# Row count of the second score matmul, and one gather and turn of the short request's rows for four experts

## The chip, the cores and the metric

The kernel runs on one core of one Trainium2 chip. The metric is the device time of one execution in microseconds (us). Below, TensorE is called PE in the profile (its weight loads PEld), VectorE DVE, ScalarE ACT, GpSimd POOL; SPq is the queue of DMA issues of SyncE.

## The reference

One encoder layer is applied to two requests that share the weights: a prompt of 256 tokens and a sample of 1024 tokens, 1024 features each. All is float32.

```
h = x @ W_in + b_in                       # 8 attention heads of 64, and 8 gMLP groups
attn = softmax over three dilated windows # = one softmax with a bias row per head
gm   = gelu(u) * (W_s LN(gelu(v)) + b)
x1   = LN(alpha * x + concat(attn, gm) @ W_out)
aff  = softmax(x1 @ w_router)             # 16 experts
gates, idx = top_k(aff.T, cap)            # cap = 32 rows (prompt), 128 rows (sample) per expert
ys   = (silu(xs @ wg) * (xs @ wu)) @ wd   # xs = x1[idx], hidden width 2816
out  = LN(alpha * x1 + scatter_add(ys * gates))
```

## The kernel before

The program is written by hand for each engine, in one fixed order, with semaphores between the engines. Its stages follow each other: input product (45 to 349 us), attention (351 to 688 us), output product with the first layer norm and the router (to about 860 us), choice of the rows for each expert (TensorE nearly idle, to 934 us), and then sixteen experts, 130 us each (942 to 3031 us), and a short end.

Float32 accuracy comes from splitting. A value is written as a high part (a rounded type, `F32R`, which TensorE takes in one pass) and a low part (the rest); ACT makes high parts by a copy, DVE low parts by a subtraction (`low`, line 920).

**Attention.** A unit is one head, one request and one tile of 128 queries; there are 80 units, per head 2 of the prompt (256 keys) and 8 of the sample (1024 keys). A head has 64 features, half of the array's 128 rows. For the even heads the high parts of q lie on partitions 0 to 63 of `q_parts` and its low parts on 64 to 127; for the odd heads the other way round. `k_high` holds the high part of k in both halves. So line 475, `q` times `k_high` with 128 rows, adds high times high and low times high in one matmul. Line 476 adds the high part of q times `k_low`, and reads only the 64 rows of one half: `q[base:base + HD]` and `k_low[base:base + HD, ...]`. A sample unit has two blocks of 512 keys, thus four matmuls: 475, 476, 475, 476; a prompt unit has two of 256 keys. In one turn n of its loop TensorE computes the scores of unit n (475, 476), turns the probabilities of unit n-2 (line 484, eight 128x128 transposes for a sample unit, two for a prompt unit) and multiplies those of unit n-3 with v (line 495, sixteen or four instructions). DVE adds the bias and takes the maximum (line 1005), ACT takes the exponential (771) and copies the turned probabilities (765), DVE normalises the output (1014, 1015). In between, ACT and DVE write the parts of q and k for the next head (746 and 920).

**Experts.** Each expert has 66 weight units of 512 KB that SP loads into a ring of 14. ACT and DVE split each into `w_parts`, and TensorE multiplies the sample request's 128 rows with them in three passes (`gate_up`, `down`), and the prompt's 32 rows with the raw float32 unit (`short_gate_up`, `short_down`; tiles of 128 rows and 32 columns). The rows of expert e+1 are turned in unit 55 of expert e: POOL has gathered 128 rows into `xs` and 32 rows into `xs_p` (named xs_prompt in the profile; the other 96 partitions are zero, line 1109), two indirect DMAs for each expert (1250, 1251). `xs_transposes` turns `xs_p` and `xs` block by block, 8 + 8 transposes (574, 575), into three banks given by `xs_banks`; ACT copies them out in six pieces (812, 813), DVE makes three low parts (`xs_low`).

Of the kernel before, what the change touches and what calls it, by code (L numbers as in the profile page):

```python
# [15 lines left out]
P = 128  # L16
# [71 lines left out]
def build(nc, a, outs):  # L88
# [10 lines left out]
    with ExitStack() as ctx:  # L99
# [73 lines left out]
        xs_parts = place("xs_parts", 32768, 2, KT, CAP_S, dt=F32R)  # L173
        xs_short = place("xs_short", 34816, KT, CAP_P)
        h_parts = place("h_parts", 35328, 2, FT, CAP_S, dt=F32R)
# [13 lines left out]
        fin = place("fin", 14336, FIN_RING, D)  # L189
        fin_stats = place("fin_stats", 19840, 2, 6)  # L190
        out_idx = place("out_idx", 20048, 2)[:, :].bitcast(U32)
        nmr = place("minus_mean_rstd", 52832, TILES)
# [47 lines left out]
        s_hT, s_hh, s_hp, s_hid = sem("hT_done"), sem("hT_high"), sem("hT_short"), sem("hT_low")  # L240
        s_gath = sem("gathered")
        s_xsT, s_xsH, s_xsL = sem("xsT_done"), sem("xs_high"), sem("xs_low")
        s_ys, s_scat = sem("ys_ready"), sem("scattered")
# [52 lines left out]
        def xs_banks(e):  # L296

            return *pair(e - 1, NC - 2), short_bank(e - 1, NC - 1)

# [86 lines left out]
        def _(pe):  # L386
# [75 lines left out]
            for n in range(NU + 3):  # L462
                if n < NU:
                    h, g, qt = units[n]
                    if n >= 2:
                        pe.wait_ge(s_scored, n - 1)
                    if qt == 0:
                        pe.wait_ge(s_sl, len(LOW_STEPS) * h + 2 * (g + 1))
                    base, t0 = HD * (h % 2), gtile[g] * P
                    q = q_parts[:, h % 2, t0 + qt * P:t0 + (qt + 1) * P]  # L470
                    for c in range(0, glen[g], 512):
                        cn = min(512, glen[g])
                        out, ks = psum[:, 2 * (n % 2) + c // 512, 0:cn], slice(t0 + c, t0 + c + cn)

                        nc.tensor.matmul(out, q, k_high[:, h % 2, ks], start=True, stop=False)  # L475
                        last = nc.tensor.matmul(out, q[base:base + HD], k_low[base:base + HD, h % 2, ks], start=False, stop=True)  # L476
                    last.then_inc(s_qk, 1)
# [90 lines left out]

            def xs_transposes(e):


                for k in range(KT):
                    bank, o0 = xs_banks(e)[k // 3], k % 3 * SLOTS
                    nc.tensor.transpose(psum[:, bank, o0:o0 + P], xs_p[:, k * P:(k + 1) * P], ident)
                    last = nc.tensor.transpose(psum[:, bank, o0 + CAP_P:o0 + SLOTS], xs[:, k * P:(k + 1) * P], ident)
                last.then_inc(s_xsT, 1)

            pe.wait_ge(s_idx, 1)
            pe.wait_ge(s_gath, 32)
            xs_transposes(0)  # L580
# [18 lines left out]
            def short_gate_up(e, end):  # L599

                first = BATCH_ENDS[BATCH_ENDS.index(end) - 1] + 1 if end > 3 else 0
                for u in range(first, end + 1, 2):
                    c, ks, _ = chunk_of(u)
                    n, slot = CHUNKS[c][1], (e * UNITS + u) % RING
                    if ks[0] == 0 and c == 1 and e:
                        pe.wait_ge(s_ys, e)
                    elif ks[0] == 0 and c != 1 and e * NC + c >= 2:
                        pe.wait_ge(s_mul_p, e * NC + c - 1 if c else e * NC)
                    for i, k in enumerate(ks):
                        for g in range(4):  # L610
                            last = nc.tensor.matmul(psum[32 * g:32 * g + 32, short_bank(e, c), 0:n // 2].rearrange("p (j f) -> p j f", j=2),  # L611
                                                    xs_short[:, k, :],
                                                    raw[:, slot:slot + 2, i * n + g * (n // 4):i * n + (g + 1) * (n // 4)],
                                                    start=k == 0, stop=k == KT - 1)
                last.then_inc(s_raw, 1)
# [37 lines left out]
            for e in range(EXPERTS):  # L653
                pe.wait_ge(s_xsL, e + 1)
                for u in range(UNITS):
                    pe.wait_ge(s_lo, e * UNITS + u + 1)
# [6 lines left out]
                    if u == XS_TURN_AT and e < EXPERTS - 1:  # L663
                        pe.wait_ge(s_hid, e * NC + NC - 1)
                        pe.wait_ge(s_hp, e * NC + NC - 1)
                        pe.wait_ge(s_mul_p, e * NC + NC)
                        pe.wait_ge(s_gath, e * 32 + 64)
                        xs_transposes(e + 1)
# [5 lines left out]
        def _(act):  # L674
# [132 lines left out]
            def xs_copy(e):  # L807
                act.wait_ge(s_xsT, e + 1)
                for b, bank in enumerate(xs_banks(e)):
                    nk = min(3, KT - 3 * b)  # L810
                    turned = psum[:, bank, 0:nk * SLOTS].rearrange("p (k c) -> p k c", k=nk)
                    nc.scalar.copy(xs_short[:, 3 * b:3 * b + nk, :], turned[:, :, 0:CAP_P])
                    last = nc.scalar.copy(xs_parts[:, HI, 3 * b:3 * b + nk, :], turned[:, :, CAP_P:SLOTS])
                last.then_inc(s_xsH, 1)

            def silu(e, c):
# [78 lines left out]
        def _(dve):  # L895
# [77 lines left out]
            def split_low(step):  # L973
# [8 lines left out]
                else:  # L982
                    low(k_low[here, h % 2, cols], kT[here, h // 2, cols], k_high[here, h % 2, cols]).then_inc(s_sl, 1)

            for step in range(len(LOW_STEPS)):
                split_low(step)
# [121 lines left out]
            nc.vector.tensor_scalar(top_idf[0:EXPERTS, :], top_idf[0:EXPERTS, :], float(L_PROMPT), None, ALU.add).then_inc(s_top, 1)  # L1108
            link(nc.vector.memset(xs_p, 0.0))
            dve.wait_ge(s_topT, 1)  # L1110
# [4 lines left out]
            nc.vector.tensor_copy(idx[:, 2, :], psum[:, 2, 32:48])  # L1115

            nc.vector.tensor_scalar(out_idx[:, 0:1], psum[:, 1, EXPERTS - 1:EXPERTS], -float(L_PROMPT), None, ALU.add).then_inc(s_idx, 1)

            def xs_low(e):
                dve.wait_ge(s_xsH, e + 1)  # L1120
                for b, bank in enumerate(xs_banks(e)):
                    nk = min(3, KT - 3 * b)
                    ks = slice(3 * b, 3 * b + nk)
                    turned = psum[:, bank, 0:nk * SLOTS].rearrange("p (k c) -> p k c", k=nk)
                    last = low(xs_parts[:, LO, ks, :], turned[:, :, CAP_P:SLOTS], xs_parts[:, HI, ks, :])
                last.then_inc(s_xsL, 1)
# [92 lines left out]
        def _(pool):  # L1219
# [108 lines left out]
```

## Time and profile before

| | |
|---|---|
| median of 3 runs | 3056.05 us (3044.93 to 3086.59) |
| profiled execution | 3055.43 us, of which span 3053.6 us |
| busy share of the span | PE 95%, PEld 73%, DVE 61%, ACT 52%, POOL 7% |
| mean granted TensorE clock | 0.963 of full speed |

The page of the profile gives busy time per engine, but a matmul's duration there contains its way through the array, and matmuls overlap. So durations of single matmuls are not their price: the price is the distance from one start to the next. The rows below come from the timeline (start, duration, engine, line, operation, output and inputs; in brackets the idle time before it and what ended it), from the table of stretches (windows), and from the groups of instructions. The row count of a matmul's stationary tile stands before the star: 64*128 is 64 rows and 128 columns. The granted clock is 1.00 at 2.4 GHz and 0.50 at 1.2 GHz.

### The profile page before, as it was taken

The page shows a single profiled execution, that of the slowest core. Times are in us where ns is not written, and L with a number is a line of the kernel's source. Part 1 is how long each engine was busy: PE and PEld are TensorE (multiplying, and loading weights), DVE is VectorE, ACT ScalarE, POOL GpSimd, SP SyncE. Part 2 cuts the span into 40 slices and gives each one's busy share as a digit, 9 for nine tenths or more (in the row PEclk, how much of TensorE's full clock was granted, in tenths as well). Part 3 has the DMA queues.
Part 4 walks back from the last instruction along what each step waited for, and adds up shares of the span by engine and source line. Part 5 has one row for each costly group of instructions (what it writes and reads, how often), then busy time and mean ns, then how long its engine had stood idle before and what let it go on. Part 6 is the DMA issues. An engine that isn't in the chain of part 4 may idle for free.

```text
span 3053.6 us, 50934 instructions
## 1 busy us (share of the span) xinstructions
PE 2903.5 (95%) x21389; PEld 2227.6 (73%) x21389; DVE 1857.0 (61%) x2261; ACT 1573.2 (52%) x2054; POOL 202.7 (7%) x167
## 2 busy tenths in 40 slices
PE   6999999998917999999999999999999999999996
PEld 6998777777715777777777777777777777777774
DVE  3531135545476666666766666666666666666688
ACT  2201346652104666665666666566665666656663
POOL 0200000000000000000000000000000000000054
PEclk8999769999958999999999999999999999999998
DMA  4100101012234787887878878788787878878794
GB/s 153 42 29 14 41 15 37 28 70 81 85 138 155 261 294 271 284 280 260 294 265 287 283 265 287 259 295 276 270 289 256 293 269 292 275 259 293 269 348 181
DMA packets 293217, 636.96 MB, mean 209 GB/s; under 512 B 22547, under 2 KB 68499, under 8 KB 292947
## 3 DMA queue, kind: packets, MB, share of 16 engines
q1 hardware_dynamic: 278544, 599.46, 55.6%
q0 software_dynamic: 9216, 26.87, 3.7%
q10 hardware_dynamic: 5228, 7.36, 0.7%
q8 instruction: 169, 2.77, 0.4%
q14 instruction: 60, 0.49, 0.0%
HBM read 607.34 MB, written 26.28 MB: 207 GB/s over the span
## 4 chain that ended last, share of the span: by engine, by line
PE 90%; DVE 6%; issue 1%; DMA 1%; ACT 0%; POOL 0%; ACTq 0%; DVEq 0%; POOLq 0%
PE banks L635 16%; PE banks L594 11%; PE banks L428 11%; PE banks L611 10%; PE banks L595 10%; PE banks L596 10%; PE banks L648 5%; PE banks L495 4%; PE banks L484 3%; PE banks L476 2%; PE banks L475 2%; PE banks L623 1%; DVE w_parts L920 1%; DMA b_s<-in_gmlp_b_s 1%; DVE top L1097 1%
## 5 line engine op out<-in xcount | busy, mean ns | idle before, releaser
L920 DVE TENSOR_TENSOR w_parts<-raw_units,w_parts 128x1024 fp32r<-128x1024 f32 x1056 | 1292.3, 1233 | 640.0 <-ACT w_parts L874 593.1
L874 ACT CAST w_parts<-raw_units 128x1024 fp32r<-128x1024 f32 x1056 | 1104.9, 1052 | 792.3 <-PE banks L596 490.0
L594 PE MATMUL banks<-w_parts,xs_parts 128*128 128x512 f32 (+1 forms) x1536 | 594.8, 387 | 6.0 <-DVE w_parts L920 6.0
L595 PE MATMUL banks<-w_parts,xs_parts 128*128 128x512 f32 (+1 forms) x1536 | 574.9, 374 | 0.0
L596 PE MATMUL banks<-w_parts,xs_parts 128*128 128x512 f32 (+1 forms) x1536 | 572.3, 373 | 0.0
L635 PE MATMUL banks<-w_parts,h_parts 128*128 128x512 f32 x2112 | 510.6, 397 | 4.0 <-DVE h_parts L920 4.0
L635 PEld LDWEIGHTS banks<-w_parts,h_parts 128*128 128x128 f32 x2112 | 390.8, 189 | 119.3 <-issue 39.8
L594 PEld LDWEIGHTS banks<-w_parts,xs_parts 128*128 128x128 f32 x1536 | 289.7, 189 | 129.1 <-issue 72.0
L611 PE MATMUL banks<-raw_units,xs_short 128*32 128x256 f32 (+1 forms) x6144 | 344.1, 364 | 0.0
L596 PEld LDWEIGHTS banks<-w_parts,xs_parts 128*128 128x128 f32 x1536 | 290.2, 189 | 52.4
L595 PEld LDWEIGHTS banks<-w_parts,xs_parts 128*128 128x128 f32 x1536 | 290.3, 189 | 44.6
L611 PEld LDWEIGHTS banks<-raw_units,xs_short 128*32 128x32 f32 x6144 | 176.2, 110 | 131.1 <-issue 44.5
L1005 DVE CUSTOM_DVE_ANT_0 scored<-banks,relT 128x1024 f32<-128x1024 f32 (+1 forms) x80 | 85.1, 1064 | 169.9 <-PE banks L476 169.6
L428 PE MATMUL banks<-win_parts,x_parts 128*128 128x256 f32 x1440 | 175.8, 286 | 4.5 <-issue 4.5
L428 PEld LDWEIGHTS banks<-win_parts,x_parts 128*128 128x128 f32 x1440 | 175.4, 195 | 4.7 <-issue 4.7
L648 PE MATMUL banks<-raw_units,h_short 128*32 128x256 f32 x2816 | 171.9, 382 | 0.0
L1262 POOL DMA_INDIRECT acc_rows<-ys,idx x15 | 31.4, 2092 | 1784.8 <-ACT ys_prompt L855 1784.8
L495 PE MATMUL banks<-v_rows,probsT 128*128 128x64 f32 x1088 | 144.7, 290 | 0.0
L495 PEld LDWEIGHTS banks<-v_rows,probsT 128*128 128x128 f32 x1088 | 142.9, 211 | 0.0
L765 ACT COPY probsT<-banks 128x1024 f32<-128x1024 f32 (+1 forms) x80 | 70.7, 884 | 134.4 <-PE banks L484 134.2
L648 PEld LDWEIGHTS banks<-raw_units,h_short 128*32 128x32 f32 x2816 | 81.8, 110 | 69.5 <-issue 25.7
L428 PE MATMUL banks<-x_parts,win_parts 128*128 128x512 f32 (+1 forms) x576 | 110.4, 354 | 0.0
(167 smaller groups left out, 2302.9 us busy)
## 6 DMA issues: line engine op xcount, KB each, us to landing
raw_units<-in_w_gate SPq DMA_DIRECT2D x352, 512.0 KB, 5.5
raw_units<-in_w_up SPq DMA_DIRECT2D x352, 512.0 KB, 6.4
raw_units<-in_w_down SPq DMA_DIRECT2D x352, 512.0 KB, 5.7
win_raw<-in_w_in SPq DMA_DIRECT2D x10, 1024.0 KB, 5.1
relT<-rel_bias SPq DMA_DIRECT2D x8, 960.0 KB, 4.3
x_rows<-x SPq DMA_DIRECT2D x10, 512.0 KB, 2.6
acc_rows<-ax SPq DMA_DIRECT2D x10, 512.0 KB, 2.6
fin<-acc_rows POOLq DMA_DIRECT2D x10, 512.0 KB, 8.0
```

The costliest lines, as they stand in the source:

```text
L428: last = nc.tensor.matmul(out, w_of(wp), x_of(xp), start=first and n == 0, stop=last_one and n == 2)
L484: last = nc.tensor.transpose(psum[:, 4 + kt // 4, kt % 4 * P:(kt % 4 + 1) * P], probs[:, m % 3, kt * P:(kt + 1) * P], ident)
L495: last = nc.tensor.matmul(psum[:, 6 + m % 2, 0:HD], probsT[:, m % 2, kt, :], v_rows[:, gtile[g] + kt, h * HD:(h + 1) * HD], start=kt == 0, ...
L594: nc.tensor.matmul(out, xs_parts[:, HI, k, :], w_hi, start=k == 0, stop=False)
L595: nc.tensor.matmul(out, xs_parts[:, LO, k, :], w_hi, start=False, stop=False)
L596: last = nc.tensor.matmul(out, xs_parts[:, HI, k, :], w_lo, start=False, stop=k == KT - 1)
L611: last = nc.tensor.matmul(psum[32 * g:32 * g + 32, short_bank(e, c), 0:n // 2].rearrange("p (j f) -> p j f", j=2), xs_short[:, k, :], raw[ ...
L635: last = nc.tensor.matmul(psum[:, pair(e, NC)[half], :], h_parts[:, h_part, f, :], w_parts[:, w_part, slot, half * 512:half * 512 + 512], ...
L648: last = nc.tensor.matmul(psum[32 * g:32 * g + 32, short_bank(e, NC), 0:QUARTER], h_short[:, f, :], raw[:, (e * UNITS + GU_UNITS + f) % RI ...
L874: nc.scalar.copy(w_parts[:, HI, n % SPLIT, :], raw[:, n % RING, :]).then_inc(s_hi, 1)
L920: return nc.vector.tensor_tensor(out, whole, high.bitcast(F32), ALU.subtract)
L1005: link(nc.vector.tensor_tensor_reduce(out=scored[:, n % 2, 0:L], in0=src, in1=bias, scale=1.0, scalar=-3e38, op0=ALU.add, op1=ALU.max, acc ...
```

## The change

In attention, `k_low` is cleared once where no low part of k is ever written (the 64 other partitions of both buffers), and line 476 takes all 128 rows of q and `k_low`. The products with the zeros add nothing.

In the experts, the rows of the short request are gathered for four experts by one indirect DMA, which fills all 128 partitions of `xs_p`; the row numbers come from a new tile `idx_four`. It is turned only ahead of experts 0, 4, 8 and 12, into two further banks, and copied whole to a larger `xs_short` of 128 columns per block, of which expert e reads the columns of its quarter. The rows of the sample are turned in blocks of four to a bank, so that ACT and DVE have two pieces where they had three. The clearing of `xs_p` goes.

```diff
         def xs_banks(e):
-            return *pair(e - 1, NC - 2), short_bank(e - 1, NC - 1)
+            return *pair(e - 1, NC - 2), pair(e - 1, NC - 1)[1], short_bank(e - 1, NC - 1)
...
                         nc.tensor.matmul(out, q, k_high[:, h % 2, ks], start=True, stop=False)
-                        last = nc.tensor.matmul(out, q[base:base + HD], k_low[base:base + HD, h % 2, ks], start=False, stop=True)
+                        last = nc.tensor.matmul(out, q, k_low[:, h % 2, ks], start=False, stop=True)
...
             def xs_transposes(e):
+                banks = xs_banks(e)
+                pe.wait_ge(s_gath, 16 * (e + 1))
                 for k in range(KT):
-                    bank, o0 = xs_banks(e)[k // 3], k % 3 * SLOTS
-                    nc.tensor.transpose(psum[:, bank, o0:o0 + P], xs_p[:, k * P:(k + 1) * P], ident)
-                    last = nc.tensor.transpose(psum[:, bank, o0 + CAP_P:o0 + SLOTS], xs[:, k * P:(k + 1) * P], ident)
+                    last = nc.tensor.transpose(psum[:, banks[k // 4], k % 4 * P:(k % 4 + 1) * P], xs[:, k * P:(k + 1) * P], ident)
+                if e % 4 == 0:
+                    pe.wait_ge(s_gath_p, 16 * (e // 4 + 1))
+                    for k in range(KT):
+                        last = nc.tensor.transpose(psum[:, banks[2 + k // 4], k % 4 * P:(k % 4 + 1) * P], xs_p[:, k * P:(k + 1) * P], ident)
                 last.then_inc(s_xsT, 1)
...
-                                                    xs_short[:, k, :],
+                                                    xs_short[:, k, e % 4 * CAP_P:(e % 4 + 1) * CAP_P],
...
                     if u == XS_TURN_AT and e < EXPERTS - 1:
                         pe.wait_ge(s_hid, e * NC + NC - 1)
-                        pe.wait_ge(s_hp, e * NC + NC - 1)
+                        pe.wait_ge(s_hp, e * NC + (NC if (e + 1) % 4 == 0 else NC - 1))
                         pe.wait_ge(s_mul_p, e * NC + NC)
-                        pe.wait_ge(s_gath, e * 32 + 64)
                         xs_transposes(e + 1)
...
             def xs_copy(e):
                 act.wait_ge(s_xsT, e + 1)
...
+                for b in range(2):
+                    last = nc.scalar.copy(xs_parts[:, HI, 4 * b:4 * b + 4, :], psum[:, banks[b], :].rearrange("p (k c) -> p k c", k=4))
                 last.then_inc(s_xsH, 1)
+                if e % 4 == 0:
+                    for b in range(2):
+                        last = nc.scalar.copy(xs_short[:, 4 * b:4 * b + 4, :], psum[:, banks[2 + b], :].rearrange("p (k c) -> p k c", k=4))
+                    last.then_inc(s_xsP, 1)
...
+            dve.wait_ge(s_job, len(jobs))
+            nc.vector.memset(k_low[HD:P, 0, :].bitcast(F32), 0.0)
+            link(nc.vector.memset(k_low[0:HD, 1, :].bitcast(F32), 0.0))
             for step in range(len(LOW_STEPS)):
                 split_low(step)
...
-            link(nc.vector.memset(xs_p, 0.0))
...
+            for g in range(4):
+                nc.vector.tensor_scalar(idx_four[32 * g:32 * g + 32, :], psum[32 * g:32 * g + 32, 2, 32 + g:48:4], -float(g), 0.25,
+                                        ALU.add, ALU.mult)
...
             def gather(e):
                 pool.indirect_dma_start(xs, None, x1_d, rows_at(0, e, P)).then_inc(s_gath, 16)
-                pool.indirect_dma_start(xs_p[0:CAP_P, :], None, x1_d, rows_at(1, e, CAP_P)).then_inc(s_gath, 16)
+                if e % 4 == 0:
+                    pool.indirect_dma_start(xs_p, None, x1_d,
+                                            bass.IndirectOffsetOnAxis(ap=idx_four[:, e // 4:e // 4 + 1], axis=0)).then_inc(s_gath_p, 16)
```

Where the order of instructions changes, it stands so. On TensorE, in unit 55 of expert 0 (between the two products of `down` and the short request's), before the change:

```order
L635 MATMUL banks<-w_parts,h_parts 128x512 x24
L574 MATMUL banks<-ident,xs_prompt 128x128
L575 MATMUL banks<-ident,xs 128x128
L574 MATMUL banks<-ident,xs_prompt 128x128
L575 MATMUL banks<-ident,xs 128x128
```

and so on to sixteen transposes. After the change, ahead of expert 1 (and of every expert that is no multiple of four):

```order
L627 MATMUL banks<-ident,hidden 128x128 x2
L628 MATMUL banks<-ident,hidden_short 64x128
L652 MATMUL banks<-raw_units,h_short 32x256 x16
L639 MATMUL banks<-w_parts,h_parts 128x512 x24
L575 MATMUL banks<-ident,xs 128x128 x8
L652 MATMUL banks<-raw_units,h_short 32x256 x16
```

The eight transposes of the short request are gone there; ahead of experts 4, 8 and 12 they stand behind the eight of the sample.

On DVE, where the input product ends and attention starts, after the change (before it, the two rows with MEMSET are not there, and the others follow in the same order):

```order
L926 TENSOR_TENSOR win_parts<-win_raw,win_parts 128x2048 x3
L993 MEMSET k_low 64x1280
L994 MEMSET k_low 64x1280
L926 TENSOR_TENSOR q_parts<-qT_first,q_parts 64x256
L926 TENSOR_TENSOR k_low<-kT,k_high 64x256
```

Two clearings of 1280 columns come ahead of the first low parts.

On POOL's queue, at the start of the experts, after the change:

```order
L1261 DMA xs<-x_rows,idx 128x1024
L1263 DMA xs_prompt<-x_rows,idx_four 128x1024
L1261 DMA xs<-x_rows,idx 128x1024
L1275 DMA acc_rows<-ys,idx 1280x1024
L1276 DMA acc_rows<-ys_prompt,idx 5120x256
L1261 DMA xs<-x_rows,idx 128x1024
```

Before it, every gather of `xs` was followed by one of 32 rows into `xs_p`; now one of 128 rows follows each fourth.

## Rows read from the trace of the kernel before

**Rows 1.** The page: the chain that ended last, shares by engine.
```profile
PE 90%; DVE 6%; issue 1%; DMA 1%; ACT 0%; POOL 0%; ACTq 0%; DVEq 0%; POOLq 0%
```

**Rows 2.** Windows: length; busy PE, PEld, DVE, ACT, POOL; clock; DMA share; GB/s.
```profile
351.10:436.50 85.40, 82.97 (x277) 61.51 (x277) 27.95 (x75) 34.95 (x56) 0.00 (x0) 0.50 0.12 42
436.50:684.00 247.50, 247.50 (x1614) 193.10 (x1614) 124.00 (x351) 151.22 (x230) 0.00 (x0) 1.00 0.11 42
934.40:937.80 3.40, 3.40 (x16) 3.21 (x16) 0.00 (x0) 0.00 (x0) 0.00 (x0) 0.50 0.00 0
937.80:942.30 4.50, 0.20 (x1) 0.03 (x1) 2.63 (x5) 4.20 (x9) 1.81 (x2) 0.88 0.46 143
942.30:948.30 6.00, 6.00 (x14) 4.74 (x15) 6.00 (x6) 4.49 (x6) 0.00 (x0) 0.50 0.01 2
950.00:2980.00 2030.00, 2028.29 (x15976) 1492.68 (x15975) 1389.74 (x1376) 1240.97 (x1558) 142.13 (x91) 1.00 0.81 279
```

**Rows 3.** Timeline, PE: one sample unit at full clock, and the next one's start.
```profile
481.91 0.48 PE L475 MATMUL banks<-k_high,q_parts 128*128 128x512 f32 x1
482.32 0.49 PE L476 MATMUL banks<-k_low,q_parts 64*128 64x512 f32 x1
...
483.61 1.09 PE L484 MATMUL banks<-ident,probs 128*128 128x128 f32 x8
...
486.24 0.48 PE L475 MATMUL banks<-k_high,q_parts 128*128 128x512 f32 x1
```

**Rows 4.** Timeline, PE: one sample unit at the low clock, and the next one's start.
```profile
376.13 0.77 PE L475 MATMUL banks<-k_high,q_parts 128*128 128x512 f32 x1
376.84 0.79 PE L476 MATMUL banks<-k_low,q_parts 64*128 64x512 f32 x1
...
384.04 0.78 PE L475 MATMUL banks<-k_high,q_parts 128*128 128x512 f32 x1
```

**Rows 5.** Timeline, PE: matmuls with 128 rows only, first expert, at either clock.
```profile
943.29 0.63 PE L596 MATMUL banks<-w_parts,xs_parts 128*128 128x512 f32 x1
943.72 0.63 PE L594 MATMUL banks<-w_parts,xs_parts 128*128 128x512 f32 x1
...
949.14 0.39 PE L596 MATMUL banks<-w_parts,xs_parts 128*128 128x512 f32 x1
949.37 0.39 PE L594 MATMUL banks<-w_parts,xs_parts 128*128 128x512 f32 x1
```

**Rows 6.** Timeline, ACT and DVE: one attention unit at full clock, with parts written.
```profile
479.06 1.05 ACT L746 CAST k_high<-kT 64x1024 fp32r<-64x1024 f32 x1
480.40 1.01 ACT L765 COPY probsT<-banks 128x1024 f32<-128x1024 f32 x1 [0.30 <-PE banks L484]
481.44 1.15 ACT L771 ACTIVATE probs<-scored,nmx 128x1024 f32<-128x1024 f32 x1
482.50 0.19 ACT L771 ACTIVATION_READ_ACCUMULATOR probs<-scored,nmx 128x1 f32 x1
483.71 1.23 DVE L1005 CUSTOM_DVE_ANT_0 scored<-banks,relT 128x1024 f32<-128x1024 f32 x1 [1.24 <-PE banks L476]
```

**Rows 7.** Timeline, PE: starts of two units, the first with four products by v.
```profile
470.25 0.48 PE L475 MATMUL banks<-k_high,q_parts 128*128 128x512 f32 x1
473.24 0.48 PE L475 MATMUL banks<-k_high,q_parts 128*128 128x512 f32 x1
```

**Rows 8.** Timeline, PE: the first matmul of attention.
```profile
351.10 0.52 PE L475 MATMUL banks<-k_high,q_parts 128*128 128x256 f32 x1 [2.42 <-DVE k_low L920]
```

**Rows 9.** Groups by form, DVE: the clearing of the short request's tile.
```profile
L1109 DVE MEMSET xs_prompt<- 128x1024 f32 x1 | 0.9, 912 | 0.2 <-issue 0.2
```

**Rows 10.** Timeline, PE: the first of sixteen transposes, and what follows them.
```profile
1052.44 0.27 PE L574 MATMUL banks<-ident,xs_prompt 128*128 128x128 f32 x1
...
1054.28 1.93 PE L648 MATMUL banks<-raw_units,h_short 128*32 128x256 f32 x32
```

**Rows 11.** Timeline, PE: the first turn of all, and the first expert's first matmul.
```profile
934.36 0.45 PE L574 MATMUL banks<-ident,xs_prompt 128*128 128x128 f32 x1 [7.52 <-DMA xs_prompt<-x_rows,idx]
...
942.30 0.77 PE L594 MATMUL banks<-w_parts,xs_parts 128*128 128x512 f32 x1 [4.30 <-DVE w_parts L920]
```

More of the change, by code:

```diff
@@ L173, in build @@
         xs_parts = place("xs_parts", 32768, 2, KT, CAP_S, dt=F32R)
-        xs_short = place("xs_short", 34816, KT, CAP_P)
+        xs_short = place("xs_short", 50368, KT, P)
         h_parts = place("h_parts", 35328, 2, FT, CAP_S, dt=F32R)
@@ L190, in build @@
         fin_stats = place("fin_stats", 19840, 2, 6)
+        idx_four = place("idx_four", 20064, 4)[:, :].bitcast(U32)
         out_idx = place("out_idx", 20048, 2)[:, :].bitcast(U32)
@@ L240, in build @@
         s_hT, s_hh, s_hp, s_hid = sem("hT_done"), sem("hT_high"), sem("hT_short"), sem("hT_low")
-        s_gath = sem("gathered")
-        s_xsT, s_xsH, s_xsL = sem("xsT_done"), sem("xs_high"), sem("xs_low")
+        s_gath, s_gath_p = sem("gathered"), sem("gathered_short")
+        s_xsT, s_xsH, s_xsL, s_xsP = sem("xsT_done"), sem("xs_high"), sem("xs_low"), sem("xs_short")
         s_ys, s_scat = sem("ys_ready"), sem("scattered")
@@ L468, in _ @@
                         pe.wait_ge(s_sl, len(LOW_STEPS) * h + 2 * (g + 1))
-                    base, t0 = HD * (h % 2), gtile[g] * P
+                    t0 = gtile[g] * P
                     q = q_parts[:, h % 2, t0 + qt * P:t0 + (qt + 1) * P]
@@ L569, in xs_transposes @@
             def xs_transposes(e):
+                banks = xs_banks(e)
+                pe.wait_ge(s_gath, 16 * (e + 1))
                 for k in range(KT):
-                    bank, o0 = xs_banks(e)[k // 3], k % 3 * SLOTS
-                    nc.tensor.transpose(psum[:, bank, o0:o0 + P], xs_p[:, k * P:(k + 1) * P], ident)
-                    last = nc.tensor.transpose(psum[:, bank, o0 + CAP_P:o0 + SLOTS], xs[:, k * P:(k + 1) * P], ident)
+                    last = nc.tensor.transpose(psum[:, banks[k // 4], k % 4 * P:(k % 4 + 1) * P], xs[:, k * P:(k + 1) * P], ident)
[3 more added lines that the diff above has]
+                        last = nc.tensor.transpose(psum[:, banks[2 + k // 4], k % 4 * P:(k % 4 + 1) * P], xs_p[:, k * P:(k + 1) * P], ident)
                 last.then_inc(s_xsT, 1)
             pe.wait_ge(s_idx, 1)
-            pe.wait_ge(s_gath, 32)
             xs_transposes(0)
@@ L654, in _ @@
                 pe.wait_ge(s_xsL, e + 1)
+                pe.wait_ge(s_xsP, e // 4 + 1)
                 for u in range(UNITS):
@@ L808, in xs_copy @@
                 act.wait_ge(s_xsT, e + 1)
[L809 to L813, printed above, removed]
+                banks = xs_banks(e)
+                for b in range(2):
+                    last = nc.scalar.copy(xs_parts[:, HI, 4 * b:4 * b + 4, :], psum[:, banks[b], :].rearrange("p (k c) -> p k c", k=4))
                 last.then_inc(s_xsH, 1)
+                if e % 4 == 0:
+                    for b in range(2):
+                        last = nc.scalar.copy(xs_short[:, 4 * b:4 * b + 4, :], psum[:, banks[2 + b], :].rearrange("p (k c) -> p k c", k=4))
+                    last.then_inc(s_xsP, 1)
             def silu(e, c):
@@ L1120, in xs_low @@
                 dve.wait_ge(s_xsH, e + 1)
[L1121 to L1125, printed above, removed]
+                for b in range(2):
+                    ks = slice(4 * b, 4 * b + 4)
+                    last = low(xs_parts[:, LO, ks, :], psum[:, xs_banks(e)[b], :].rearrange("p (k c) -> p k c", k=4), xs_parts[:, HI, ks, :])
                 last.then_inc(s_xsL, 1)
```

## The prediction, made before the changed kernel ran

> **What bounds the kernel now.** I read the chain that ended last first: 90% of it is TensorE [rows 1], so work taken from TensorE shortens the end, wherever TensorE does not wait. Then the windows: from 436.5 to 684 us, most of attention, TensorE is busy for every microsecond at clock 1.00, and from 950 to 2980 us, the experts, for 2028 of 2030 us [rows 2]. DVE and ACT are busy for 50 and 61% in the first stretch, for 68 and 61% in the second. One thing stands out: from 351.1 to 436.5 us the clock is 0.50, though TensorE counts as busy for 83 of the 85.4 us [rows 2]. Last the timeline, since busy time hides what matters here.
>
> A sample unit at full clock takes 486.24 - 481.91 = 4.33 us. Its four score matmuls take 483.61 - 481.91 = 1.70 us, 0.425 us from start to start [rows 3]. Matmuls of the same width and type that all have 128 rows start every 0.23 us (949.14, 949.37) [rows 5]; I take 0.227, the mean over a run of them. So each of the four loses 0.2 us. At the low clock a unit takes 384.04 - 376.13 = 7.91 us with scores at 0.71 to 0.72 [rows 4], where the all-128-row stream has 0.43 [rows 5]: 0.29 us lost each. What differs is that 128 rows and 64 rows alternate. The Trainium skill (TensorEngine Tiling (Array Packing), Key Properties) says that a change of the tiling mode drains TensorE; the trace agrees, with 0.2 us at each change.
>
> **Part 1: scores with 128 rows.** Four matmuls at 0.227 instead of 0.425 save 0.79 us per sample unit, and two save 0.40 us per prompt unit. A head has 8 and 2 of them: 7.1 us; eight heads 57 us. The fourth change of mode, to the transposes behind the scores, is in it, because the 1.70 us ends at the first transpose. The added 64 rows cost nothing by themselves: the distance goes by columns, and the 128-row matmul of line 475 is as long as the 64-row one of line 476 (0.48 and 0.49) [rows 3].
>
> Not all of the 57 us need arrive, for the new unit takes 4.33 - 0.79 = 3.54 us, and ACT in a unit with a 1024-wide part needs 1.05 + 1.01 + 1.15 + 0.19 = 3.40 us [rows 6]. It just fits; DVE had 1.24 us idle in its unit [rows 6] and loses 0.79 of them. But in each head two units have only four products by v instead of sixteen; one lasts 473.24 - 470.25 = 2.99 us [rows 7] and becomes 2.2 us, below ACT's 3.40. The other is shorter still, but ACT has less to do in it. TensorE then waits, by ACT's lag less what its lead gives back. Bounds per head: 0 us (ACT works off its lag in the units without parts, where it needs 2.35 us) and 3 us (both short units last as long as ACT's, and DVE's order adds some). I take 1 us, since an exponential is needed only two units later: 8 us over eight heads.
>
> **Part 2: the low clock at the start of attention.** It costs now 85.4 x (1 - 4.33/7.91) = 38.7 us. What did TensorE do before the clock rose elsewhere? From 934.4 to 937.8 us it ran 16 transposes back to back at 0.50, and then stood at 0.88 on average over the next stretch; from 942.3 to 948.3 it ran dense 128-row matmuls at 0.50, and was at 1.00 after [rows 2]. In attention at the low clock the scores of a unit are not dense: 0.43 us of streaming in 0.72 [rows 4, 5]. With the change a low-clock unit has 4 x 0.43 = 1.7 us of dense scores, then about as long of transposes without a change of mode between them: as much dense work in a row as preceded the rise after 934.4. So I expect the clock to come up in the first few sample units. As an estimate I take 20 us of low clock from the first matmul. A low-clock unit is then 7.91 - 4 x 0.29 = 6.75 us, so the stretch costs 20 x (1 - 3.54/6.75) = 9.5 us. Gain: 29 us. Bounds: the low clock is gone within 5 us (gain 36), or lasts as long as now (cost 85.4 x 0.476 = 40.6, a loss of 2).
>
> **Part 3: the clearing of k_low.** Two MEMSETs of 1280 columns; one of 1024 takes 0.91 us [rows 9], so 2.3 us on DVE ahead of the first low parts, and DVE can only start when the input product ends. TensorE's first matmul waits for k_low [rows 8] and moves by about 1.2 us, because DVE had waited for ACT's high parts anyway. But then TensorE waits for the first maximum, which comes behind the sample's low parts, and these wait for ACT's copies (to about 352.5 us), which are not moved. I take 0; if the cover fails it is 2.3 us.
>
> **Part 4: the turns of the short request.** Sixteen transposes take 1054.28 - 1052.44 = 1.84 us [rows 10], so eight about 0.87 us. They go ahead of 12 of the 16 experts (not 0, 4, 8, 12): 10.4 us. TensorE is the bound there [rows 2], so it all counts. ACT has one block of six copies fewer in those, DVE two subtractions for three; both have room and are taken at nothing. The new wait for `s_hp` ahead of experts 4, 8 and 12 asks for the last hidden copy of ACT, which ACT does behind the split of unit 57, free to run when TensorE has done unit 51; between that and unit 55 lie four `down` units of 1.4 us and one short product, so it is long done. If not, it would be below 2 us three times. Behind it on TensorE stands everything, so it would count in full. Gathering 128 rows in one DMA instead of 32 four times moves the same bytes, issued an expert ahead: nothing.
>
> At the first turn the gather is on the path: TensorE waits 7.52 us for the `xs_p` rows, and starts the experts at 942.30, held by DVE's low part [rows 11]. Now `xs` can be turned while `xs_p` is under way, the clearing (0.91 us [rows 9]) goes, four tiny index operations come, `xs_p` has four times the rows, and ACT copies `xs_short` in two blocks of 512 behind what DVE needs. Bounds: 1.5 us gained, 2 us lost. I take 0.
>
> **The sum.** The profiled execution took 3055.4 us (span 3053.6), 0.6 below the median of the three runs. 3055.4 - 57 + 8 - 29 - 10.4 = 2967 us. The spread of the three runs, 3045 to 3087 us, is of the size of the low stretch's cost, so I think its length varies from run to run; that is not shown by this trace.
>
> **The rivals.**
> - *The low clock stays as long.* For it: TensorE counted as busy in it too, and the products by v (line 495) are unchanged. Against: the rise after transposes alone. Then 3055.4 - 57 + 8 + 2 - 10.4 = 2998 us. The Trainium skill (TensorE: Matmul & The Clock Gate, Part 4) says that transposes don't count as busy for the clock; by that rule this rival would be likely. This trace does not agree: 16 transposes alone, 934.4 to 937.8 us, were followed by a rise [rows 2].
> - *ACT and DVE become the bound in attention.* At 3 us lost per head, 16 more than in my sum: 2983 us. For it: 3.40 against 3.54 us; against: most units have no 1024-wide part.
> - *The change does not do what it says:* the pause belongs to something else that the scores do, such as sharing q as the stationary tile or the switch of banks. Against: the experts' three passes share tiles as well and have no pause [rows 5]. Then only part 4 is left: 3045 us.
> - *Slower:* tighter scores let TensorE wait for ACT in small pieces, and the clock stays at 0.50 for all of attention. Each of the 64 sample units is then 6.75 instead of 3.54 us: 205 us more than at full clock, 196 more than in my sum, 3163 us. It turns from gain to loss when the low stretch costs more than 38.7 + 59 = 98 us, that is after 98/0.476 = 206 us of low clock. Against: from 436.5 us on the clock held at 1.00 with the pauses of today [rows 2], and the new units are denser.
>
> **How the numbers follow.** My forecast 0.58, the low clock as long 0.20, ACT and DVE 0.12, no effect on the scores 0.05, slower 0.05. The predicted time is 2967 us. The low end is the forecast without any wait for ACT (8 us), with the low clock gone in 5 us (7) and the first turn's gain: 2950, and some for the spread of runs, 2945. The high end takes in the rival with the long low clock, 2998, and a few us of unknown costs: 3003. About 2% is what a measurement of this kernel can tell from no change: 2995 us is that line. Faster by over 2%: 0.58 + 0.12 and 0.08 of the 0.20 that lies at the line, 0.78. Within 2%: 0.12 + 0.05 = 0.17. Slower: 0.05.
>
> **What would show it.** The score matmuls start every 0.23 us at full clock and the first transpose follows at the same pace; if they stay at 0.43, part 1 is wrong. A full unit takes 3.5 to 3.6 us. In the windows, the clock reaches 1.00 before 375 us; if it is still 0.50 at 420, part 2 is wrong. TensorE's idle time ahead of lines 475 and 484, put down to ACT's exponential or copy, shows the wait: 8 us in all, not 24. An expert that is no fourth takes 0.87 us less than 130.1 us, and no idle time stands ahead of the turns at unit 55. The prediction fails if the clock behaves otherwise than after the two rises in [rows 2], in either direction.

## The result, and the profile after

The changed kernel takes 2967.1 us (median of 4 runs, 2966.6 to 2967.9); the kernel before took 3050.5 us in the runs beside it (3041 to 3087). The ratio is 0.975, 95% interval 0.971 to 0.979: 2.5% faster. (The two medians alone give 0.973; the ratio is taken over the fast runs.) One thing shows before any trace is opened: the runs of the kernel before spread over tens of us, those of the changed one over 1.2 us.

The page of the changed kernel, its first line, then the lines of the clock and of the chain, which answers to [rows 1]:

```profile
span 2964.8 us, 50663 instructions
...
PEclk9999999999769999999999999999999999999998
...
PE 88%; DVE 7%; DMA 1%; issue 1%; ACT 1%; POOL 0%; ACTq 0%; SPq 0%; DVEq 0%; POOLq 0%
```

TensorE is the bound as before. Where the time went is read from the table of stretches. The stretches run from the first score matmul to the first transpose of the concatenated rows (attention), from there to the first matmul of the experts, through the experts to DVE's last sums (`ys`), and to the end. The columns are start and end, length, busy time and count on PE, PEld, DVE, ACT and POOL, granted clock, DMA share and GB/s. Before:

```profile
351.10:688.12 337.02, 334.02 (x1920) 258.02 (x1920) 152.84 (x430) 187.18 (x286) 0.00 (x0) 0.87 0.11 41
688.12:942.30 254.18, 159.81 (x829) 132.05 (x830) 148.81 (x231) 44.47 (x67) 11.77 (x24) 0.82 0.26 97
942.30:3032.20 2089.90, 2084.14 (x16356) 1534.30 (x16360) 1445.65 (x1428) 1276.21 (x1600) 169.76 (x110) 1.00 0.81 277
3032.20:3053.60 21.40, 0.91 (x16) 0.26 (x8) 11.31 (x16) 0.00 (x0) 4.57 (x6) 0.62 0.09 31
```

After:

```profile
352.00:610.27 258.27, 248.19 (x1921) 230.68 (x1921) 152.43 (x430) 185.26 (x284) 0.00 (x0) 0.99 0.15 52
610.27:864.38 254.11, 160.02 (x830) 131.80 (x830) 148.58 (x233) 44.71 (x65) 10.99 (x23) 0.81 0.27 98
864.38:2944.40 2080.02, 2073.63 (x16260) 1522.34 (x16264) 1444.45 (x1413) 1276.76 (x1546) 157.22 (x99) 1.00 0.81 278
2944.40:2964.80 20.40, 0.93 (x16) 0.27 (x10) 11.31 (x16) 0.00 (x0) 4.56 (x6) 0.64 0.09 32
```

Attention is 78.8 us shorter, the experts 9.9 us, the end 1.0 us; the middle is the same to 0.1 us. As the first score matmul comes 0.9 us later, that is 88.8 us of span. In attention the mean clock went from 0.87 to 0.99. The low stretch of [rows 2], 85 us long before, is at most 7.5 us long now (the first four matmuls, to 352.5 us, still had the clock at 1.00, hence the mean of 0.54):

```profile
352.00:359.50 7.50, 5.30 (x18) 4.05 (x19) 5.01 (x12) 5.46 (x10) 0.00 (x0) 0.54 0.86 280
359.50:607.00 247.50, 240.19 (x1883) 224.07 (x1881) 146.52 (x415) 179.58 (x275) 0.00 (x0) 1.00 0.13 46
```

And the timeline of TensorE at full clock, to be held against [rows 3] (a sample unit and the next one's start; lines 477 and 478 are the old 475 and 476):

```profile
450.39 0.48 PE L477 MATMUL banks<-k_high,q_parts 128*128 128x512 f32 x1
450.71 0.39 PE L478 MATMUL banks<-k_low,q_parts 128*128 128x512 f32 x1
450.94 0.40 PE L477 MATMUL banks<-k_high,q_parts 128*128 128x512 f32 x1
451.17 0.39 PE L478 MATMUL banks<-k_low,q_parts 128*128 128x512 f32 x1
451.40 0.38 PE L486 MATMUL banks<-ident,probs 128*128 128x128 f32 x2
```

The four score matmuls take 1.01 us where they took 1.70. They start 0.23 us apart, but the first takes 0.32 us, behind the products by v. A full sample unit, from 366.65 to 370.25 us, takes 3.60 us instead of 4.33.

### The profile page after: what moved, and what is told of

Same layout as the page of the kernel before. It is cut to its first block, busy times and chain, and to the rows that moved or that the text cites. A ratio compares the mean times of both kernels' runs of the same rounds, so it can differ in the third digit from the quotient of the medians.

```text
span 2964.8 us, 50663 instructions
## 1 busy us (share of the span) xinstructions
PE 2806.2 (95%) x21293; PEld 2186.2 (74%) x21293; DVE 1857.5 (63%) x2250; ACT 1573.3 (53%) x1998; POOL 189.4 (6%) x155
## 4 chain that ended last, share of the span: by engine, by line
PE 88%; DVE 7%; DMA 1%; issue 1%; ACT 1%; POOL 0%; ACTq 0%; SPq 0%; DVEq 0%; POOLq 0%
PE banks L639 17%; PE banks L598 12%; PE banks L430 11%; PE banks L615 11%; PE banks L599 10%; PE banks L600 10%; PE banks L652 5%; PE banks L497 4%; PE banks L486 2%; DVE w_parts L926 1%; PE banks L627 1%; PE banks L477 1%; PE banks L478 1%; DMA b_s<-in_gmlp_b_s 1%; DVE top L1107 1%
## 5 line engine op out<-in xcount | busy, mean ns | idle before, releaser
L497 PE MATMUL banks<-v_rows,probsT 128*128 128x64 f32 x1088 | 130.2, 271 | 0.0
L497 PEld LDWEIGHTS banks<-v_rows,probsT 128*128 128x128 f32 x1088 | 127.8, 192 | 0.0
L430 PE MATMUL banks<-wout_hi,catT_parts 128*128 128x512 f32 x320 | 106.0, 401 | 4.2 <-DVE wout_lo L926 4.2
```

Source lines behind the costliest of these rows:

```text
L430: last = nc.tensor.matmul(out, w_of(wp), x_of(xp), start=first and n == 0, stop=last_one and n == 2)
L497: last = nc.tensor.matmul(psum[:, 6 + m % 2, 0:HD], probsT[:, m % 2, kt, :], v_rows[:, gtile[g] + kt, h * HD:(h + 1) * HD], start=kt == 0, ...
```

## The experiments

Three questions: what each half of the change is worth by itself; whether the pause at each score matmul belongs to the change of the row count; and why the clock comes up now. Each run stood beside runs of the kernel before on its chip, whose medians were 3047 to 3056 us with runs from 3026 to 3116 us. A ratio to them is therefore loose, and I compare the times with each other and read the traces.

**1. The scores alone.**

```diff
-                        last = nc.tensor.matmul(out, q[base:base + HD], k_low[base:base + HD, h % 2, ks], start=False, stop=True)
+                        last = nc.tensor.matmul(out, q, k_low[:, h % 2, ks], start=False, stop=True)
...
+            nc.vector.memset(k_low[HD:P, 0, :].bitcast(F32), 0.0)
+            link(nc.vector.memset(k_low[0:HD, 1, :].bitcast(F32), 0.0))
```

> The kernel before with line 476 on 128 rows and the two clearings, and nothing of the experts' part. Theory: attention gives the whole gain but for the turns. In the two traces attention (first score matmul to first transpose of the concatenated rows) went from 337.0 to 258.3 us, and the experts gave about 10. So 2966.6 + 10 = 2977 us, and the low clock ends within some 10 us of the first score matmul. Rival: the experts' part also removes waits of the first turn or of POOL, then it is worth more and this run is above 2985 us.

Measured: 2979.1 us (2977.7 to 2979.9), ratio 0.978 (0.971 to 0.985). The clock is at 1.00 from 362 us on. So the attention half brings the gain but for 12 us, and the small spread comes with it.

**2. The turns alone.** The changed kernel with the line above put back and the clearings out.

> The changed kernel with line 476 back on 64 rows and without the clearing of k_low. Theory: 10.4 us below the kernel before of the same low stretch, that is 3031 to 3047 us, spread by tens of us from run to run as the kernel before is, with the low clock in attention for tens of us. An expert that is no fourth takes 0.87 us less. Rival: if the low stretch in attention were ended by anything else of the change, it would be short here too and the time near 3010 us.

Measured: 3050.7 us, 3016 to 3104 in ten runs; ratio 0.998 (0.992 to 1.004). My range for the median was missed: ten runs reach further than I thought, and 10 us can't be seen in such a spread. The trace can tell, because its low stretch happens to end at about the same place as in the trace of before (437 and 436.5 us):

```profile
352.00:432.00 80.00, 77.44 (x261) 57.87 (x261) 25.64 (x69) 31.78 (x51) 0.00 (x0) 0.50 0.13 44
436.00:680.00 244.00, 244.00 (x1575) 189.16 (x1576) 123.07 (x348) 149.68 (x228) 0.00 (x0) 1.00 0.11 39
```

This execution's span is 3042.7 us, against 3053.6: 10.9 us less at the same low stretch. The rival is out; the low clock is untouched by the turns.

**3. Both 128-row matmuls first, then both 64-row ones.**

```diff
                         nc.tensor.matmul(out, q, k_high[:, h % 2, ks], start=True, stop=False)
+                    for c in range(0, glen[g], 512):
+                        cn = min(512, glen[g])
+                        out, ks = psum[:, 2 * (n % 2) + c // 512, 0:cn], slice(t0 + c, t0 + c + cn)
                         last = nc.tensor.matmul(out, q[base:base + HD], k_low[base:base + HD, h % 2, ks], start=False, stop=True)
```

> The kernel before with the four score matmuls of a unit in another order: both with 128 rows first, then both with 64 rows, so the row count changes twice in a unit's scores and the way out, not four times. Theory (the pause belongs to each change of the row count): 475 to 475 and 476 to 476 start 0.23 us apart, 475 to 476 and 476 to the first transpose 0.43, a sample unit at full clock takes 4.33 - 0.40 = 3.93 us, attention gains 8 x 8 x 0.4 = 26 us plus what the clock gives. Rival A (a matmul with 64 rows is slow in itself, or the one behind it): 476 to 476 stays at 0.43 and the unit gains 0.2 us at most. Rival B (the pause comes from two matmuls on one bank in a row): all four at 0.23, since banks now alternate, 0.79 us per unit.

Measured: 3003.4 us (3001.7 to 3031.5). In the timeline (x2 is two matmuls in one row) the unit takes 3.94 us:

```profile
481.89 0.71 PE L475 MATMUL banks<-k_high,q_parts 128*128 128x512 f32 x2
482.54 0.73 PE L479 MATMUL banks<-k_low,q_parts 64*128 64x512 f32 x2
483.19 1.09 PE L487 MATMUL banks<-ident,probs 128*128 128x128 f32 x8
...
485.83 0.71 PE L475 MATMUL banks<-k_high,q_parts 128*128 128x512 f32 x2
```

Two matmuls take 0.65 us on either side of the change, which is the sum that the theory gave, but not 0.23 and 0.43: listed singly, the first two start at 481.89 and 482.21 us, and the third at 482.54. Each of them takes 0.32 to 0.33 us. So the 0.2 us of a change is split: about 0.1 us falls on the matmul ahead of it and 0.1 us on the one behind. (In the changed kernel 0.32 us is what the first score matmul behind the products by v takes, and the others take 0.23.) A 64-row matmul is not slower than a 128-row one beside the same change, which speaks against rival A, and two banks in turn did not bring all four to 0.23, against rival B. Half the changes, half the gain of full clock. In the trace the clock was at 0.50 to about 367 us and at 1.00 from 368 us, 16 us after the first score matmul, where the kernel before took 85 us in its trace, with the same matmuls in another order; the one run at 3031.5 us suggests that it may come up later.

**4. All score matmuls with 64 rows.** `q` and `k_high` in line 475 are cut to `[base:base + HD]` too. This leaves out the product of q's low part and k's high part, so the scores are less exact.

> The kernel before with line 475 on 64 rows too (the product of q's low part and k's high part is left out, so the scores are less exact). All four score matmuls then have 64 rows, and the row count changes once into the scores and once out of them. Theory: inside the scores 0.23 us from start to start at full clock, 0.43 at the low clock; only the step to the first transpose keeps its 0.43, and the way from the products by v may gain 0.2. A sample unit takes 4.33 - 0.6 + up to 0.2 = 3.7 to 3.95 us. Rival: 64 rows are slow in themselves; then all four stay at 0.43.

Measured: 3184 us in the one run, 4.5% above the median of the kernel before. Inside the scores the pause is gone, as expected, but that is at the low clock, and the low clock holds through almost the whole of attention (windows; timeline of PE):

```profile
352.00:776.00 424.00, 420.71 (x1626) 361.80 (x1625) 136.05 (x377) 165.59 (x253) 0.00 (x0) 0.50 0.08 30
778.00:812.00 34.00, 34.00 (x251) 29.60 (x251) 15.94 (x49) 18.66 (x28) 0.00 (x0) 1.00 0.10 32
...
485.92 0.63 PE L476 MATMUL banks<-k_low,q_parts 64*128 64x512 f32 x1
486.35 0.62 PE L475 MATMUL banks<-k_high,q_parts 64*128 64x512 f32 x1
486.77 0.63 PE L476 MATMUL banks<-k_low,q_parts 64*128 64x512 f32 x1
```

Starts 0.43 us apart at 0.50 of the clock: this is as dense as the changed kernel is at the low clock. By my reason for part 2 ("the scores of a unit are not dense") the clock should have come up within the first units. It did not. It came up at about 777 us, beside the last head's prompt units and still with 64-row scores, so such scores put the rise off but do not rule it out. My reason is not the whole one, and the next runs are about it.

**5. Head 0 with 64 rows, the rest as changed.**

```diff
-                    t0 = gtile[g] * P
+                    base, t0 = HD * (h % 2), gtile[g] * P
...
-                        last = nc.tensor.matmul(out, q, k_low[:, h % 2, ks], start=False, stop=True)
+                        if h > 0:
+                            last = nc.tensor.matmul(out, q, k_low[:, h % 2, ks], start=False, stop=True)
+                        else:
+                            last = nc.tensor.matmul(out, q[base:base + HD], k_low[base:base + HD, h % 2, ks], start=False, stop=True)
```

> The changed kernel, but with 64 rows in line 478 for the first head's units (ten of 80). Theory (the low clock ends because the scores are dense): it stays at 0.50 through all or most of head 0, some 55 us, and comes up in the first units of head 1, which are dense. Time: eight sample units at 7.91 instead of 3.59 us at most, 2967 + 15 to 40 = 2982 to 3007 us, with little spread if the rise always waits for head 1. Rival (the rise within 8 us was luck of that run or comes from something else, such as the later start): the clock is up before 375 us, and the time is 2967 + 8 x 0.75 = 2973 us.

Measured: 2995.9 us (2992.3 to 2997.6). The clock stays low through all ten units of head 0 and comes up in the first unit of head 1:

```profile
404.03 3.51 PE L500 MATMUL banks<-v_rows,probsT 128*128 128x64 f32 x16
407.30 0.56 PE L477 MATMUL banks<-k_high,q_parts 128*128 128x256 f32 x1
407.66 0.41 PE L479 MATMUL banks<-k_low,q_parts 128*128 128x256 f32 x1
407.87 1.91 PE L489 MATMUL banks<-ident,probs 128*128 128x128 f32 x8
...
411.93 0.36 PE L477 MATMUL banks<-k_high,q_parts 128*128 128x256 f32 x1
412.13 0.28 PE L479 MATMUL banks<-k_low,q_parts 128*128 128x256 f32 x1
```

At 407.66 the 256-column matmuls are still 0.21 us apart; at 411.93 the second 128-row unit runs at full speed. One head of 64-row seconds costs 29 us, of which the pauses at full clock would be 8 x 0.7 = 6. The rest is the clock.

**6. Head 0 with 128 rows, the rest as before.** The condition turned round (`h == 0`), in the kernel before.

> The kernel before with 128 rows in line 476 for the first head's units only, and the clearings; the other seven heads alternate as before. Theory: the clock comes up in the first units of head 0 and holds, since the kernel before held it at 1.00 with alternating rows from 436.5 us on; so this one head brings the clock's gain of 29 to 35 us and a seventh to an eighth of the rest, 5 us: 3055 - 38 = about 3017 us, and the spread of the runs is small (below 5 us). Rival (the alternating rows let the clock fall again): low stretches in later heads, spread of tens of us, time above 3030 us.

Measured: 3016.8 us (3015.4 to 3017.9 in eight runs), ratio 0.990 (0.987 to 0.993). The table of stretches:

```profile
352.00:360.00 8.00, 5.75 (x22) 4.51 (x22) 5.52 (x12) 5.94 (x12) 0.00 (x0) 0.57 0.73 249
360.00:640.00 280.00, 279.22 (x1832) 219.64 (x1831) 145.28 (x411) 176.33 (x270) 0.00 (x0) 1.00 0.11 38
```

Ten units of 80 take the low stretch and the spread of the runs away, and the alternating scores of the other seven heads hold the full clock. So bringing the clock up and holding it are two things.

**7. All four with 128 rows, half of them times zero.** In the changed kernel the second copy of k's high part is written as zeros, so q's low part is multiplied by zeros only.

```diff
-                nc.scalar.copy(dst, src).then_inc(s_sh, 1)
+                if what == "k again":
+                    nc.scalar.mul(dst, src, 0.0).then_inc(s_sh, 1)
+                else:
+                    nc.scalar.copy(dst, src).then_inc(s_sh, 1)
```

> The changed kernel with the second copy of k's high part written as zeros (the product of q's low part and k's high part is thereby left out, as in the run with all matmuls on 64 rows, and the scores are the same numbers as there). All four score matmuls have 128 rows, half of them with zeros. With all matmuls on 64 rows the scores were as dense (0.43 us from start to start at the low clock) and the clock stayed at 0.50 for all of attention. Theory (the number of rows that a matmul takes counts for the clock, whatever the data): the clock is up within some 10 us, as in the changed kernel, 2967 us. Rival (density in time would have been enough and that run's low clock was chance, or the data of the rows counts): low clock for all or much of attention, 3050 us or more.

Measured: 2967.2 us (2964.2 to 2967.9), the time of the changed kernel, and the clock is up before 360 us:

```profile
352.00:360.00 8.00, 5.71 (x22) 4.48 (x21) 5.51 (x12) 5.92 (x13) 0.00 (x0) 0.57 0.71 239
360.00:600.00 240.00, 232.66 (x1814) 216.53 (x1814) 143.09 (x407) 174.89 (x267) 0.00 (x0) 1.00 0.12 43
```

The scores are the same numbers as in experiment 4, equally dense; in attention only the row count of the instructions differs, and with it the two changes of row count per unit that experiment 4 has. Experiment 3 also has two changes per unit, with two of its four matmuls on 128 rows, and its clock was up by 368 us, so two changes alone do not keep the clock low. For the rise the rows that a matmul takes count, then, and not what lies in them. Density may count as well: experiment 3 is the kernel before with half the changes, and three of its four runs lie within 2.3 us of each other; whether fewer changes made its clock rise early is not shown, since the runs of the kernel before differ so much.

**8. Experiment 4 again, several times, and with head 0 on 128 rows.**

> The same kernel as the run with all score matmuls on 64 rows (q's low part times k's high part left out), timed several times. Theory (64-row scores can't bring the clock up, however dense): each run is near 3184 us, with the low clock through all of attention. Rival (chance): the runs spread from about 2990 to 3184 us.

> The kernel before with both score matmuls on 128 rows in head 0 and both on 64 rows in heads 1 to 7 (where the product of q's low part and k's high part is left out). Theory: the dense 128-row units of head 0 bring the clock up, and 64-row scores then hold it, since the kernel before held it with every second matmul on 64 rows: full clock from about 362 us on, a sample unit of 3.75 to 3.95 us in heads 1 to 7, about 2998 us. Rival (64-row scores let it fall again): 0.50 in later heads, above 3080 us.

Measured: 3212 us for 64 rows everywhere (3157 to 3216), and 2994.4 us (2993.9 to 2996.0) with head 0 on 128 rows. The first shows that the low clock of experiment 4 was no chance. In its trace the clock is 0.50 up to the last score matmul (829.55 us) and comes up 13 us later, when TensorE has only the last transposes and products by v to do, all with 128 rows:

```profile
352.00:829.00 477.00, 473.63 (x1829) 407.30 (x1828) 149.32 (x417) 182.76 (x280) 0.00 (x0) 0.50 0.08 27
...
844.00:846.00 2.00, 2.00 (x19) 1.94 (x18) 0.45 (x2) 0.00 (x0) 0.00 (x0) 1.00 0.00 0
```

The second shows that 64-row scores hold a full clock once they have it (starts 0.23 us apart, 0.33 to the transposes):

```profile
479.69 0.49 PE L478 MATMUL banks<-k_high,q_parts 64*128 64x512 f32 x1
480.03 0.39 PE L482 MATMUL banks<-k_low,q_parts 64*128 64x512 f32 x1
480.26 0.39 PE L478 MATMUL banks<-k_high,q_parts 64*128 64x512 f32 x1
480.49 0.39 PE L482 MATMUL banks<-k_low,q_parts 64*128 64x512 f32 x1
480.82 1.09 PE L490 MATMUL banks<-ident,probs 128*128 128x128 f32 x8
```

Ten units with 128 rows at the start are worth about 160 to 220 us between these two kernels.

**9. ACT's wide parts one turn later, and two of DVE's low parts with them.** In the trace of after, TensorE waits in attention only for this (waits of PE, 352 to 605 us; total, times, longest):

```profile
PE banks L486 <- ACT probsT L769: 7.3, 7, 1.2
PE banks L477 <- DVE k_low L926: 3.9, 1, 3.9
PE banks L477 <- DVE nmx L1017: 2.2, 1, 2.2
```

Once in each of seven heads, ACT writes a 1024-wide part just when the turned probabilities need to be copied:

```profile
457.25 1.05 ACT L750 CAST k_high<-kT 64x1024 fp32r<-64x1024 f32 x1
...
458.32 1.01 ACT L769 COPY probsT<-banks 128x1024 f32<-128x1024 f32 x1
...
459.48 1.06 PE L486 MATMUL banks<-ident,probs 128*128 128x128 f32 x8 [1.14 <-ACT probsT L769]
```

```diff
+        HIGH_AT, LOW_AT = (1, 2, 3, 5, 6, 7), (4, 5, 7, 8)
...
-                if h + 1 < HEADS and 1 <= i <= len(HIGH_STEPS):
-                    split_high(len(HIGH_STEPS) * (h + 1) + i - 1)
+                if h + 1 < HEADS and i in HIGH_AT:
+                    split_high(len(HIGH_STEPS) * (h + 1) + HIGH_AT.index(i))
...
-                if h + 1 < HEADS and 4 <= i < 4 + len(LOW_STEPS):
-                    split_low(len(LOW_STEPS) * (h + 1) + i - 4)
+                if h + 1 < HEADS and i in LOW_AT:
+                    split_low(len(LOW_STEPS) * (h + 1) + LOW_AT.index(i))
```

> The changed kernel with ACT's three 1024-wide parts of the next head one turn later (turns 5, 6, 7 of a head, not 4, 5, 6) and DVE's two at turns 7 and 8. Theory: in the trace of after TensorE stands 1.0 to 1.2 us in each of seven heads at line 486 behind ACT's copy of the probabilities, because the wide part of turn 4 is ahead of that copy. Without it the wait is 0.2 us or less: 7 x 1.0 = 7 us, 2960 us. Rival: the wait moves to another turn, since ACT has 3.40 us of work in a 3.59 us unit, and the time stays within 2 us of 2967.

Measured: 2960.1 us (2958.4 to 2961.4 in six runs), ratio to before 0.972 (0.967 to 0.976), below every run of the changed kernel. The wait behind `probsT` is not in the list any more. A head took 31.87 us (prompt units' first matmuls at 444.59 and 476.46 us) and takes 30.68 us (443.55 and 474.23). This version beats both kernels.

## Why the prediction was right, point by point

The time was forecast as 2967 us and is 2967.1. The agreement to 0.1 us is luck: two of its parts were off by 6 to 7 us in opposite directions.

- **The pause belongs to the change of the row count.** Right, by experiment 3 and by the 64-row scores of experiment 8, though it lies half ahead of the change and half behind it. The distance fell to 0.23 us as read from [rows 5].
- **57 us for the scores, 8 of them lost to ACT.** The mechanism was right, the size was off. The step that failed is "four matmuls at 0.227": the first of four takes 0.32 us, so a unit gained 0.73 us (4.33 to 3.60), not 0.79. With prompt units and the waits a head went from 37.1 to 31.87 us, 5.2 us, so 42 us over eight heads, where the sum had 57 - 8 = 49. The first matmul explains about 5 of the 7 us (0.06 us in each of 64 sample units and, as an estimate, 0.07 in each of 16 prompt units).
- **TensorE waits for ACT in the short units.** Right in size and nearly in place: 7 waits, 7.3 us, where I took 8, each in the turn right behind the two short ones (459.48 us follows the short turns that start at 453.32 and 454.92); experiment 9 gave 7 us back.
- **29 us from the clock.** The direction was right. The size: from the end of the input product (348.7 us before, 348.1 after) to the end of attention 77.2 us were saved, and 42 of them are the heads' shorter period, so by this estimate about 35 us are the clock's. The stretch of low clock lasted 7.5 us, not the 20 I took; the gain came near the better of my two bounds, 36. The reason that I gave for it, dense scores, was only half of it. Experiments 4 and 8 have dense scores with 64 rows and a low clock for over 400 us; experiment 7 has 128 rows and a rise within 8. The other half of my reason, that the transposes take part in a rise, was not tested by itself; what bears on it is the end of attention with 64 rows everywhere (experiment 8), where the clock rose under transposes and products by v alone.
- **Nothing for clearing k_low.** Nearly: the first score matmul came 0.9 us later, TensorE's idle time ahead of it grew from 2.42 [rows 8] to 3.9 us, and the sample's first unit started at 354.98 us, no later than before (355.58). DVE began the sample's low parts at 351.92 us, just as ACT's copy of q landed (350.85 + 1.04), so the clearing took time in which DVE had waited for ACT before (1.57 us).
- **10.4 us for the turns.** Right: 9.9 us in the experts, and 10.9 us of span by experiment 2. The turn ahead of expert 1 took 974.23 - 973.26 = 0.97 us with eight transposes, where sixteen took 1.84 [rows 10]. No idle time stands ahead of the turns; the added wait cost nothing.
- **Nothing at the first turn.** Right: TensorE waited 6.9 us for `xs` and 0.2 us for `xs_p`, where it waited 7.52 us [rows 11], and ACT's copies took the rest: 1.92 us (859.98 to 861.90) ahead of its first expert part, where they took 1.37 (938.10 to 939.47).
- **The spread of the runs is the low stretch.** I had said that the trace did not show it. It is supported now. Every kernel whose trace has the clock up within 17 us of the first score matmul has runs within 4 us, but for one run of experiment 3; experiment 5, whose stretch of 58 us ends with head 0, has them within 6 us; and the two that alternate rows from the start (before, and the turns alone) spread over 80 us and more. The mean granted clock of a whole run of the kernel before goes with its time: 0.973 at 3026 us, 0.962 at 3058, 0.943 at 3116.
- **The slower rival,** low clock for all of attention, was put at 3163 us, if it came. Its price was about right: experiment 4, which has that clock, took 3184 and 3157 to 3216 us. Its cause, small waits for ACT, did not work: the clock held at 1.00 with 7.3 us of such waits.

## What to carry to other kernels

Read the distance from start to start, not the busy time: TensorE counted as busy for every microsecond while 40% of the scores' time (1.70 against 1.01 us) was pause. Rows that multiply zeros can be cheaper than leaving them out, when leaving them out changes the shape of the tile between neighbours. And where the clock is low at the start of a stage, look at what TensorE does in the stage's first units, and try full 128-row matmuls there: here ten units decided about 30 us, and in the all-64-row version 160 us or more.

## What the runs showed of the hardware that was not expected

- The granted clock does not come up by density in time alone. Score matmuls 0.43 us apart at 1.2 GHz, streaming without pause, left it at 0.50 for 424 us with 64 rows, and had it at 1.00 within 8 us with 128 rows (experiments 4 and 7). Half of the 128 rows multiplied zeros, so it is not the data. Nor is it the rows of the scores alone: with 64 rows the clock came up at 777 us in one trace, in the other at 843 us, when the scores had ended. What decides the moment stays open.
- The low stretch is entered at the start of attention. The clock was at 1.00 in the first matmuls after (352.00 to 352.50 us) and at 0.50 from 353 us on, with TensorE idle for 3.93 us ahead of them and 2.20 us behind; before, it fell between 351 and 352 us, behind 2.42 us of idle time.
- Once at 2.4 GHz, the same 64-row matmuls held it, for 278 us at a mean of 0.99 (experiment 8), and so did alternating ones, for 280 us (experiment 6).
- A change of the row count between 128*128 and 64*128 tiles costs 0.2 us at 2.4 GHz, about half on the matmul ahead of it and half on the one behind (experiments 3 and 8: 0.32 to 0.33 us where the stream has 0.23; 0.43 us for a matmul that has a change on both sides, [rows 3]). At 1.2 GHz a matmul with a change on both sides takes 0.72 us where the stream has 0.43 [rows 4, 5].
- The first score matmul behind the products by v takes 0.1 us more than the others also where the row count does not change (0.32 us after). What it waits for there was not looked into.
